# Loading the mixer's first rows and splitting its first weights in another order

## The reference, cut to what matters

```
y_a   = silu(layer_norm(conv(a))) @ conf_out_w + conf_out_b        # convolution branch
y_b   = y @ ssm_out_w                                              # y: (tokens, 2048), normalised
gates = sigmoid(gate_logit + gate_b)                               # (tokens, 2, 1024)
out   = (gates[:, 0] * y_a + gates[:, 1] * y_b) @ w_o
```

## Time and profile before

| what | us |
| --- | --- |
| median of 3 executions | 1598.5 (1597.82 to 1607.12) |
| the profiled execution's own time | 1598.62 |
| its span, first to last instruction | 1596.9 |
| TensorE busy in the span | 1378.5 (86%) |
| VectorE busy | 1175.7 (74%) |
| ScalarE busy | 813.0 (51%) |
| POOL busy | 212.3 (13%) |
| granted TensorE clock, mean | 0.92 |

### The profile page before, as it was taken

The page is one execution under the profiler, slowest core; times in us unless marked ns, Lnnn a source line. Parts: engine busy times, 40 slices in busy tenths (PEclk is TensorE's granted clock), DMA queues, the critical chain, the costliest instruction groups (busy, mean ns, idle before and its releaser), DMA issues. The chain is left out here.

```text
span 1596.9 us, 25982 instructions
## 1 busy us (share of the span) xinstructions
PE 1378.5 (86%) x8618; PEld 1219.4 (76%) x8618; DVE 1175.7 (74%) x1634; ACT 813.0 (51%) x1427; POOL 212.3 (13%) x328
## 2 busy tenths in 40 slices
PE   4989899998999989999892899997359999999980
PEld 4988888888888888888881799985348777777760
DVE  4557987888878788887876454542748999999964
ACT  4353554534545345462541332322138999999961
POOL 1011030210202102021120000000201111111112
PEclk9988998999999899998995999999669999999995
DMA  6141624426144261442713824311678999999936
GB/s 190 52 115 55 188 63 121 114 78 177 47 121 113 72 184 47 136 108 80 192 42 123 249 66 161 116 53 34 267 278 305 361 368 367 370 365 367 369 113 237
DMA packets 191724, 273.98 MB, mean 172 GB/s; under 512 B 15661, under 2 KB 154117, under 8 KB 175252
## 3 DMA queue, kind: packets, MB, share of 16 engines
q1 hardware_dynamic: 179100, 248.36, 46.7%
q0 software_dynamic: 9536, 17.98, 3.2%
q10 hardware_dynamic: 3040, 7.03, 1.2%
HBM read 238.21 MB, written 52.48 MB: 182 GB/s over the span
## 5 line engine op out<-in xcount | busy, mean ns | idle before, releaser
L868 PE MATMUL pu<-xh,wh 128*128 128x304 f32 (+1 forms) x1280 | 294.9, 313 | 31.3 <-DVE wl L237 29.1
L868 PE MATMUL pu<-xl,wh 128*128 128x304 f32 (+1 forms) x1280 | 282.2, 303 | 0.0
L868 PE MATMUL pu<-xh,wl 128*128 128x304 f32 (+1 forms) x1280 | 281.5, 303 | 0.0
L868 PEld LDWEIGHTS pu<-xh,wh 128*128 128x128 f32 x1280 | 210.2, 202 | 47.6 <-DVE wl L237 36.0
L868 PEld LDWEIGHTS pu<-xl,wh 128*128 128x128 f32 x1280 | 210.2, 201 | 0.0
L868 PEld LDWEIGHTS pu<-xh,wl 128*128 128x128 f32 x1280 | 209.0, 200 | 0.0
L1003 DVE SCALAR_TENSOR_TENSOR cacc<-a_p,gc,cacc 128x528 f32<-128x528 f32 x232 | 188.4, 812 | 5.8
L526 ACT ACTIVATE wh<-ring 128x1024 fp32r<-128x1024 f32 x80 | 84.5, 1057 | 211.1 <-PE pu L868 207.2
L1713 DVE TENSOR_TENSOR W13l<-W,W13h 128x1024 fp32r<-128x1024 f32 x160 | 185.0, 1217 | 7.0 <-issue 6.5
L1697 ACT ACTIVATE W13h<-W 128x1024 fp32r<-128x1024 f32 x160 | 156.3, 1064 | 0.2 <-issue 0.2
L2132 PE MATMUL eh<-W13h,xch 128*128 128x512 f32 x320 | 130.5, 408 | 14.7 <-DVE xcl L2219 10.2
(11 more groups left out here) (394 smaller groups left out, 2644.0 us busy)
## 6 DMA issues: line engine op xcount, KB each, us to landing
W<-in_exp_w SPq DMA_DIRECT2D x100, 1024.0 KB, 7.2
ring<-in_w_in SPq DMA_DIRECT2D x80, 512.0 KB, 4.1
x<-in_exp_w SPq DMA_DIRECT2D x20, 1024.0 KB, 7.7
stage<-decay_rows SPq DMA_DIRECT2D x8, 1120.0 KB, 6.6
x<-in_state_ssm SPq DMA_DIRECT2D x16, 512.0 KB, 6.3
out_new_ssm_sample<-x SPq DMA_DIRECT2D x16, 512.0 KB, 5.3
wraw<-in_ssm_out_w SPq DMA_DIRECT2D x8, 1024.0 KB, 7.4
Ed<-decay_rows SPq DMA_DIRECT2D x32, 140.0 KB, 6.9
```

The lines of the kernel that those rows point to most:

```text
L868: last = pe.matmul(u_cols(r, a, b), w[:, k % RING, j, :], x[:, j, a:b], start=(j == 0 and n == 0), stop=(j == KD - 1 and n == 2))
```

## The change

Three things, all at the border between trunk and mixer.

1. The row blocks 0 and 1 are loaded while the trunk ends, into columns 2048 to 4287 of `x1`, and the mixer reads them there. SP issues these two loads behind `results_out(G - 1)` and ahead of `conv_out(G - 1)`, after waiting for the last states (`s_hs`) and for the rows of the groups up to the seventh (`s_yst`). The mixer loads the other six into the three slots.
2. The high and low halves of the first weight block are made in four pieces of 512 columns, one ahead of each two row blocks. TensorE waits for each piece.
3. POOL loads the first gates only when the last row block has landed.

```diff
+EARLY = 2
+
+def early_rows(x1, n):
+    flat = x1[:, :, :].rearrange("p t d -> p (t d)")
+    return flat[:, 2 * D + 2 * T * n:2 * D + 2 * T * n + 2 * T].rearrange("p (i t) -> p i t", i=2)

 # trunk, SP, after the last group
             results_out(G - 1)
+            sp.wait_ge(s_hs, 4 * G + 1)
+            sp.wait_ge(s_yst, 16 * (G - 1) + 1)
+            for n in range(EARLY):
+                sp.dma_start(early_rows(keep["x1"], n), keep["yrows"][n].rearrange("i p t -> p i t")).then_inc(s_early, 16)
             conv_out(G - 1)
+            sp.wait_ge(s_early, 16 * EARLY)
             sp.wait_ge(s_wraw, 32)

 # mixer
+        def y_rows(n):
+            return early_rows(x1, n) if n < EARLY else yraw[:, n % YR]
+        def yr_count(n):
+            return 16 * ((n - EARLY) // YR + 1)
+        def quarter(c):
+            return slice(4 * P * c, 4 * P * c + 4 * P)

 # SP
-            for n in range(KD):
-                if n >= YR:
+            for n in range(EARLY, KD):
+                if n >= EARLY + YR:
                     sp.wait_ge(s_yl, n - YR + 1)

 # POOL
+            pool.wait_ge(s_yr[(KD - 1) % YR], yr_count(KD - 1))
             for n in range(2 * KD):

 # TensorE, product
-                pe.wait_ge(s_vl, m + 1)
+                if m:
+                    pe.wait_ge(s_vl, m + 1)
                 for j in range(K):
+                    if m == 0 and j % 4 == 0:
+                        if j < 12:
+                            pe.wait_ge(s_vl0, j // 4 + 1)
+                        else:
+                            pe.wait_ge(s_vl, 1)

 # ScalarE
-            high(0)
             for n in range(KD):
-                act.wait_ge(s_yr[n % YR], 16 * (n // YR + 1))
-                act.activation(yh[:, 2 * n:2 * n + 2, :], yraw[:, n % YR], ACT.Copy).then_inc(s_yh, 1)
+                if n % 2 == 0:
+                    act.activation(vh[:, 0, quarter(n // 2)], wraw[:, 0, quarter(n // 2)],
+                                   ACT.Copy).then_inc(s_vh0 if n < KD - 2 else s_vh, 1)
+                if n >= EARLY:
+                    act.wait_ge(s_yr[n % YR], yr_count(n))
+                act.activation(yh[:, 2 * n:2 * n + 2, :], y_rows(n), ACT.Copy).then_inc(s_yh, 1)

 # VectorE
-            low(0)
             for n in range(KD):
+                if n % 2 == 0:
+                    if n < KD - 2:
+                        dve.wait_ge(s_vh0, n // 2 + 1)
+                    else:
+                        dve.wait_ge(s_vh, 1)
+                    q = quarter(n // 2)
+                    rest(vl[:, 0, q], wraw[:, 0, q], vh[:, 0, q]).then_inc(s_vl0 if n < KD - 2 else s_vl, 1)
                 dve.wait_ge(s_yh, n + 1)
-                rest(yl[:, 2 * n:2 * n + 2, :], yraw[:, n % YR], yh[:, 2 * n:2 * n + 2, :]).then_inc(s_yl, 1)
+                rest(yl[:, 2 * n:2 * n + 2, :], y_rows(n), yh[:, 2 * n:2 * n + 2, :]).then_inc(s_yl, 1)
```

More of the change, by code:

```diff
@@ L191, in trunk @@
             sem, ("s_xh", "s_xl", "s_wdh", "s_wdl", "s_wh", "s_wld", "s_ast", "s_yst", "s_wraw"))
-        s_h0 = sem("s_h0")
+        s_h0, s_early = sem("s_h0"), sem("s_early")
         s_st_conf, s_st_h, s_st_pk, s_st_pa, s_st_hp = map(
@@ L1365, in mixer @@
                 "m_tan", "m_act", "m_ya", "m_gfree", "m_mg", "m_o", "m_x1", "m_ssq", "m_var", "m_sd"))
+        s_vh0, s_vl0 = sem("m_vh0"), sem("m_vl0")
         s_lin, s_rinv, s_sqf, s_ss, s_ac, s_wo = map(sem, ("m_lin", "m_rinv", "m_sqf", "m_ss", "m_ac", "m_wo"))
```

## The result

The changed kernel takes 1592.67 us (median of 8, 1585.68 to 1595.82) against 1599.95 (median of 8). The ratio is 0.9938 with a 95% interval of 0.9916 to 0.9959: a difference clear of the noise and under one per cent, 7.3 us by the medians. The ratio is estimated from all the executions and not from the two medians; its interval stands for 6.6 to 13.4 us. Of these 5.3, 0.5 came ahead of the mixer's start, 2.9 between that start and the sums over aconv, where the change acts, and the rest, 1.8 of it in the last stage, behind it.

The account below looks back on a forecast made before the run. The mixer was taken as TensorE's own work from the second product on, delayed by waiting for loaded rows. Trunk 0 and second product's start -6.9 took 1598.5 to 1591.5 us; terms gave 1590.5 to 1592.3, full range 1589 to 1598.

Parts of the forecast that it names:

- Early loads cost nothing: Trunk's end: two row loads beside VectorE's convolution taps cost zero, bound +0.2 us.
- TensorE starts 3.3 us sooner: Mixer's start: TensorE's first matmul comes at 872.9 instead of 876.17, 3.3 us sooner.
- Rows 3 and 4 under 2 us apart: Mixer's row loads: without the gates rows 3 and 4 land 1.7 us apart, at 875.2 and 876.9.
- The last row takes 4.77 us: Row 7, issue to use: 4.77 us, so the second product starts at 889.85 against 896.76, 6.9 us sooner.
- Slower, by the clock: Rival, chance 0.05: TensorE's clock drops before the second product, which takes 25 us for 12.45; 1604 us.
- Gates behind the rows: Mixer's loads: gates share the engines with the rows; their 1.15 MB takes 3.3 us, so later gates bring rows sooner.
- pieces: First weight block in four: 0.6 and 0.5 us more in all, but only the first piece precedes the first row.
- What is late next: Behind the second product: aconv, gates and third weight block each have at least 6 us to spare.
- Rows still late: Rival, chance 0.14: latency spaces rows 3 and 4, second product at 893.7; gain 3, 1595.5 us.
- nothing: Rival, chance 0.08: something thought slack (aconv, third block, first gate) has none; 1598.5, or down to 1597 us.
- more: Rival, chance 0.09: last row returns in 3.35 us, gain 8.3, 1590 us, or 1589 with quicker rows ahead.

Follow-up runs that it names:

- second set: Six more executions of the unaltered changed kernel, against the kernel before beside it: median 1588.87 us, ratio 0.9931 (0.9914 to 0.9948).
- first profile: The changed kernel's first profiled execution, against the kernel before: 1593.31 us, second product at 21.72 us and sums over aconv at 36.60 from the mixer's start.
- profile with the clock kept: Second profile of the changed kernel, unaltered: second product at 20.79 us, sums over aconv at 33.26; median of its six executions 1588.87 us.
- run with the longer idle time: Changed kernel with the second weight block's low half computed twice, lengthening TensorE's last idle time before the second product: 1597.47 us (one execution).
- pool of five: Changed kernel with aconv behind the last row and both early places in x1 reused for later rows: medians 1589.50 and 1587.74 us, ratios 0.9937 and 0.9923.

## Why the prediction was right, and where it wasn't

The forecast, 1591.5 with 1589 to 1598, holds the 1592.67 measured, and 7 us was the difference of the medians. The second set doesn't fit as well: its median, 1588.87, is just under the range and 12.0 us under the kernel before beside it. By its steps:

- *Early loads cost nothing*: right to 0.1 us. VectorE's taps took the same, the loads lay in the idle stretch, and they are the part that moves the second product.
- *TensorE starts 3.3 us sooner*: right to a tenth (3.16 us after the mixer's start, 3.2 worked out). *Rows 3 and 4 under 2 us apart*: right (5.52 and 7.08 against 5.5 and 7.2). Rows 5 and 6 at 9.89 and 12.64, worked out as 10.8 and 12.6.
- *The last row takes 4.77 us*: mis-sized. It took 6.52 and 5.40. My upper bound was 5.3, half a microsecond over a single row of before; one landing was taken for the spread of all. The estimate of 3.3 us by the Trainium skill (DMA: Bandwidth & Descriptors, Anatomy of one DMA) is further off: no profile shows such a row used less than 3.6 us after its issue. That section gives its figures for transfers that GpSimd issues, and these go over SP's queue. The second product came at 21.72 and 20.79 us, not 20.15: gains of 5.3 and 6.3 against 6.9. The bounds beside it were also added up 0.2 us too wide: gains of 6.4 and 7.8 give 1592.1 and 1590.7.
- *Slower, by the clock*: this rival, given 0.05, is what the first profile shows in part, and its price and its point were both wrong. I let the clock stay down for the whole product; it came back within it, and the cost was 2.4 us and not 12.45. I set the point at an idle time over 1.97 us, since before kept its clock over that; it fell behind 1.02 and 1.90 us. So the longest idle time alone doesn't decide it. I also worked out wrongly what a late row does: I let 0.7 us lift the idle time ahead of the second product from 1.3 to 2.0, but a late row 7 moves its own matmuls too, and that idle time stays (0.96 in the profile with the clock kept). What grows is the one ahead of row 7's matmuls, 0.83 and 1.90 us. The Trainium skill's warning of waits between short bursts (TensorE: Matmul & The Clock Gate, HAM oscillation), which I had set aside, is nearer to what happened than my reading was: in the run with the longer idle time the clock fell in the wait of 3.28 us and the product began at 0.50. The changed kernel's first profile differs from it, since there the clock fell 1.3 us into a burst, behind a shorter wait.
- *Gates behind the rows* and *pieces*: the landings moved as worked out, but I let them reach the end in one sum without asking what each is worth alone. Behind three slots the experiments give them zero to 1.7 us and zero to 1 us at the second product. Had I worked out the sum with one part left out, as the free slot of row 7 allows, I would have seen that.
- *What is late next*: right. The third block's high half began at 898.05, TensorE needed it at 913, the first gate was there at 893.0, and no new wait of TensorE appeared.
- *Rows still late*, *nothing* and *more*: the landings refute the first, the stage times the second; the third was not reached, no last row came back in under 4.3 us.

The agreement of 7.0 with 7.3 is better than the reasoning deserves: the stage of the profiled execution gave 2.9 us at the sums, that of the second one 6.3, and the totals carry a scatter of several microseconds that none of my terms contains. That the total came out at 7.3 is in part luck: at least a microsecond of it, and more in the second set, has no source in the stage that the change touches.

## What to carry to other kernels

When loads run through a ring of slots, write down for each load which split frees its place. An early load can be worth a whole trip through the ring (5.3 us here), while starting the consumer sooner or clearing the engines moves the stage little until the ring is no longer the bound; places used once for early loads can join the ring. Idle times of one to two microseconds of TensorE close together can cost the clock, in some executions and not in others, and so take back part of what an earlier start has won. And where a kernel's total scatters by as much as the change is worth, measure the change in the stage it acts on, from that stage's own start.

## What the runs showed of the hardware that I had not expected

- TensorE's clock fell to 0.50 behind idle times of 1.02 and 1.90 us (20.25 us after the mixer's start), behind 1.25 and 2.12 (at 20.35), and within one of 3.28 behind 1.31 and 1.43 (at 23.1). It was kept over 1.97, 1.26, 0.53 and 0.95 in the kernel before, over 1.76 and 0.37, over 1.11, 0.83 and 0.96, and over 0.88, 0.37, 1.12, 1.13 and 0.98 in the kernel without early rows. Neither the longest idle time nor their sum tells the two lists apart. The price of a fall was 2.4, 0.6 and 2.6 us in a product of 12.47.
- A 0.57 MB load took 4.3 to 6.6 us from issue to use when a 2.2 MB load was issued 0.4 us behind it on the same queue, and 3.6 to 5.2 us when none was and at most one other row was on its way.
- The routing's 124 matmuls took 25.2 and 17.1 us of TensorE in two profiles of one kernel, the pool of five, by whether the clock rose there, 8 us of the total.
